# Half of x turned ahead of the last products at three borders, and two orders changed in the first mixer

## The reference

```python
# first block, layers l = 0, 1
mod = silu(c) @ w_ada[l] + b_ada[l]                    # six vectors of 1024: shift, scale, gate, twice
h = rms_norm(x, norm_mix[l]) * (1 + scale_m) + shift_m
x = x + gate_m * hybrid_mixer(h, w_in[l], ..., w_out[l])   # stick-breaking attention and gated linear attention
h = rms_norm(x, norm_ffn[l]) * (1 + scale_f) + shift_f
x = x + gate_f * hierarchical_moe(h, ...)              # 32 experts, top 2 of the best group
# second block, layers l = 0, 1
h = rms_norm(x, norm1_g[l])
x = x + concat(mla, diff, window, neighborhood attention of h @ w_in[l]) @ w_out[l]
h = rms_norm(x, norm2_g[l])
x = x + square(relu(h @ w_up[l])) @ w_down[l]
# at the end
return rms_norm(x, final_norm_g)
```

## Time and profile before

| | us |
|---|---|
| median of 3 runs | 1474.45 |
| lowest, highest | 1472.7, 1476.99 |
| profiled execution | 1473.16 |
| its span, first to last instruction | 1471.0 |
| PE busy in it | 1314.5 (89%) |
| DVE busy | 729.7 (50%) |
| ACT busy | 526.3 (36%) |
| moved by DMA | 392.08 MB |

### The profile page before, as it was taken

One profiled execution on the slowest core, in us unless ns is written; L12 is line 12 of the kernel. 1 busy time (PEld: TensorE's weight loads), 2 busy tenths in 40 slices (PEclk: granted clock), 3 DMA queues, 4 the chain that ended last, 5 costly groups with the idle time before them and its releaser, 6 DMA issues. The chain is left out here.

```text
span 1471.0 us, 21544 instructions
## 1 busy us (share of the span) xinstructions
PE 1314.5 (89%) x9066; PEld 978.5 (67%) x9066; DVE 729.7 (50%) x1126; ACT 526.3 (36%) x894; POOL 49.7 (3%) x46
## 2 busy tenths in 40 slices
PE   5999997866689999976776999999999999999997
PEld 2766774433347667642432878789998978799986
DVE  1744652211157367421111777765545777765554
ACT  3535331000045344200001546553443546644343
POOL 0200000000002000000000110000000110000000
PEclk9999999898799999998878999999999999999999
DMA  9798899999977958999999705455655405455551
GB/s 353 289 334 306 313 422 419 421 421 421 384 286 286 336 206 322 415 420 422 421 378 413 193 10 175 144 173 188 201 191 159 107 14 188 144 172 193 183 199 42
DMA packets 135976, 392.08 MB, mean 267 GB/s; under 512 B 26817, under 2 KB 40129, under 8 KB 111297
## 3 DMA queue, kind: packets, MB, share of 16 engines
q1 hardware_dynamic: 132128, 389.48, 71.1%
q10 hardware_dynamic: 3744, 1.15, 0.4%
HBM read 389.45 MB, written 1.05 MB: 265 GB/s over the span
## 5 line engine op out<-in xcount | busy, mean ns | idle before, releaser
L419 DVE TENSOR_TENSOR spl<-ring,spl 128x2048 fp32r<-128x2048 f32 x65 | 149.0, 2292 | 135.7 <-ACT spl L410 135.7
L543 PEld LDWEIGHTS ps<-hh,spl 128*128 128x128 f32 x1728 | 204.1, 189 | 6.9 <-issue 5.8
L543 PE MATMUL ps<-hh,spl 128*128 128x256 f32 x1728 | 206.2, 280 | 2.8 <-DVE hh L505 2.8
L410 ACT ACTIVATE spl<-ring 128x2048 fp32r<-128x2048 f32 x66 | 126.6, 1919 | 148.4 <-PE ps L543 107.8
L2343 PE MATMUL ps<-spl,ur 128*128 128x512 f32 x768 | 176.7, 389 | 0.0
L2343 PEld LDWEIGHTS ps<-spl,ur 128*128 128x128 f32 x768 | 143.2, 188 | 29.2
L1344 PE MATMUL ps<-ring,ar 128*32 128x256 f32 x928 | 99.4, 444 | 57.1 <-issue 24.2
L932 DVE TENSOR_TENSOR spl<-ring,spl 128x1024 fp32r<-128x1024 f32 (+2 forms) x120 | 138.2, 1175 | 23.3 <-ACT spl L923 22.9
L1344 PE MATMUL ps<-spl_as_slots,ar 128*32 128x256 f32 x864 | 106.8, 497 | 42.1 <-DMA spl_as_slots<-in_w_up 27.1
L923 ACT ACTIVATE spl<-ring 128x1024 fp32r<-128x1024 f32 (+2 forms) x120 | 116.7, 1010 | 44.3 <-PE ps L523 10.7
L523 PE MATMUL ps<-spl,hh 128*128 128x512 f32 x480 | 117.7, 398 | 4.5 <-DVE spl L932 2.1
(11 more groups left out here) (370 smaller groups left out, 1753.8 us busy)
## 6 DMA issues: line engine op xcount, KB each, us to landing
ring<-in_w_up SPq DMA_DIRECT2D x52, 1024.0 KB, 5.3
spl_as_slots<-in_w_down SPq DMA_DIRECT2D x50, 1024.0 KB, 15.2
ring<-in_w_ada SPq DMA_DIRECT2D x48, 1024.0 KB, 7.5
spl_as_slots<-in_w_up SPq DMA_DIRECT2D x40, 1024.0 KB, 16.6
ring<-in_w_gate SPq DMA_DIRECT2D x38, 1024.0 KB, 17.2
ring<-in_w_down SPq DMA_DIRECT2D x38, 1024.0 KB, 4.9
ring<-in_w_in SPq DMA_DIRECT2D x34, 1024.0 KB, 7.3
ring<-in_w_out SPq DMA_DIRECT2D x16, 1024.0 KB, 8.4
```

The source lines that it names most:

```text
L410: sc.activation(t.hi, t.raw, ACT.Copy).then_inc(s_hi, 2)
L419: v.tensor_tensor(t.lo, t.raw, t.hi, ALU.subtract).then_inc(s_lo, 1)
L543: ins = pe.matmul(ps[:, banks[m // 2], (m % 2) * 256:(m % 2) * 256 + 256], le, ri, start=(kk == 0 and q == 0 and m % 2 == 0), stop=(kk == ...
```

## The change

The order strings: in the first mixer, PE's `5155345053` becomes `5134055553` and ACT's `6350054` becomes `0063554` (DVE's is unchanged). In mixer 2 of layer 1, PE's begins with `0040004` in place of `0400040`. The first moves the first half of the ninth tile ahead of the two steps of modulation block 9 on PE, the second its split ahead of three other ACT steps. In `tiles_mix1`, `tiles_cols` is written out, and block 9's tiles come between the two tiles of block 4.

The diff without these strings and without the removed `tiles_cols`:

```diff
@@ -274,13 +270,17 @@
...
             for n, c in enumerate(IN1):
-                tiles_cols(("in", l, c), win, 512 * c, 512)
+                for half in range(2):
+                    tile(("in", l, c, half), [rows(win, 512 * c, 512, 4 * half, 4)], 4, 512)
+                    if l == 0 and n == 4 and half == 0:
+                        tiles_ada(0, [9])
...
                         out_tile(b - 10)
-                    tiles_ada(al, [b])
+                    if (al, b) != (0, 9):
+                        tiles_ada(al, [b])
@@ -480,8 +480,10 @@
...
 
-        def pe_x_T(pe, event):
-            for k2 in range(4):
+        FIRST, LAST = (0, 1), (2, 3)
+        def pe_x_T(pe, event, part=FIRST + LAST):
+            for k2 in part:
@@ -490,28 +492,42 @@
...
 
-        def act_hT(sc, g, gain, last, n):
-            for k2 in range(4):
+        def act_hT(sc, g, gain, part=FIRST + LAST, shift=0):
+            for k2 in part:
...
                 for k in (2 * k2, 2 * k2 + 1):
-                    ins = sc.activation(hT[0][:, k, :], ps[:, k2, k % 2 * 256:k % 2 * 256 + 256], ACT.Identity, scale=gain[:, k:k + 1])
+                    ins = sc.activation(hT[0][:, (k + shift) % 8, :], ps[:, k2, k % 2 * 256:k % 2 * 256 + 256], ACT.Identity, scale=gain[:, k:k + 1])
                 ins.then_inc(s_st, 1)
-            act_hi(sc, last, n)
-        def dve_hT(v, g, gain, last, n):
-            for k2 in range(4):
+        def dve_hT(v, g, gain, part=FIRST + LAST, shift=0):
+            for k2 in part:
...
                 for k in (2 * k2, 2 * k2 + 1):
-                    ins = v.scalar_tensor_tensor(hT[1][:, k, :], ps[:, k2, k % 2 * 256:k % 2 * 256 + 256], gain[:, k:k + 1], hT[0][:, k, :],
+                    h = (k + shift) % 8
+                    ins = v.scalar_tensor_tensor(hT[1][:, h, :], ps[:, k2, k % 2 * 256:k % 2 * 256 + 256], gain[:, k:k + 1], hT[0][:, h, :],
...
                 ins.then_inc(s_hT, 1)
-            if n:
-                dve_lo(v, last, n)
-        def pe_cols(pe, g, key, cn, banks, fresh=False):
+        def pe_cols(pe, g, key, cn, banks, fresh=False, early=False):
...
                 t = T[(*key, half)]
+                if fresh and early and half == 0:
+                    for k, i in ((0, 0), (1, 0), (0, 1), (1, 1), (2, 0), (3, 0), (2, 1), (3, 1)):
+                        if i == 0 and k % 2 == 0:
+                            pe.wait_ge(*g(s_hT))
+                        if (k, i) == (0, 1):
+                            pe.wait_ge(s_staged, 2)
+                        if i == 0 and k == 2:
+                            pe.wait_ge(s_lo, t.m + 1)
+                        pr = parts3([u[:, k, i * 128:(i + 1) * 128] for u in hT], [u[:, k, :] for u in t.parts])
+                        for q, (le, ri) in enumerate(pr):
+                            ins = pe.matmul(ps[:, banks[i], 0:cn], le, ri, start=(k == 0 and q == 0), stop=False, skip_group_check=True)
+                        if (k, i) == (3, 0):
+                            yield
+                    ins.then_inc(s_used, 1)
+                    yield
+                    continue
@@ -529,16 +545,18 @@
...
 
-        def pe_colsT(pe, g, key, banks, fresh=False):
+        def pe_colsT(pe, g, key, banks, fresh=False, shift=0, event=None):
...
                 for m in range(4):
+                    if event and half == 0 and m == 2:
+                        pe_x_T(pe, event, LAST)
...
                             pe.wait_ge(*g(s_hT))
-                        pr = parts3([u[:, k, m * 128:(m + 1) * 128] for u in t.parts], [u[:, kk, :] for u in hT])
+                        pr = parts3([u[:, k, m * 128:(m + 1) * 128] for u in t.parts], [u[:, (kk + shift) % 8, :] for u in hT])
@@ -722,7 +740,7 @@
...
                 lane = pe_colsT(pe, g, ("in", l, 3), [sink_bank(n, 0), sink_bank(n, 1)], fresh=(n == 0)) if c == 3 else pe_cols(
-                    pe, g, ("in", l, c), 512, [sink_bank(n, 0), sink_bank(n, 1)], fresh=(n == 0))
+                    pe, g, ("in", l, c), 512, [sink_bank(n, 0), sink_bank(n, 1)], fresh=(n == 0), early=(l == 0))
@@ -1800,6 +1818,8 @@
...
                 for m, (cols, o) in enumerate(chunks):
+                    if l and n == 0 and half == 0 and m == 2:
+                        pe_x_T(pe, 6, LAST)
@@ -1828,6 +1848,8 @@
...
                     for i in range(2):
+                        if t == 3 and c and i:
+                            pe_x_T(pe, 5 + 2 * l, FIRST)
@@ -1955,8 +1977,8 @@
...
         def pe_mix2(pe, g, l):
-            pe_x_T(pe, 4 + 2 * l)
             if l == 0:
+                pe_x_T(pe, 4)
@@ -2083,9 +2105,12 @@
...
             last = T["up2", l, 0, 1]
-            act_hT(sc, g, PR(f"n1{l}"), last, 1)
+            act_hT(sc, g, PR(f"n1{l}"), LAST if l else FIRST + LAST)
+            act_hi(sc, last, 1)
...
             for c in range(2):
+                if c:
+                    act_hT(sc, g, PR(f"n2{l}"), FIRST, 4)
@@ -2270,7 +2295,8 @@
...
             dve_ms(v, g, (3, 1))
-            dve_hT(v, g, PR(f"n1{l}"), last, 0)
+            if l == 0:
+                dve_hT(v, g, PR("n10"))
@@ -2279,6 +2305,8 @@
...
             v.tensor_reduce(m2.lam[:, 0:2], m2.tl.rearrange("p (a b) -> p a b", b=32), AX.X, ALU.add).then_inc(s_dl, 1)
+            if l:
+                dve_hT(v, g, PR("n11"), LAST)
@@ -2293,6 +2321,7 @@
...
                     else:
+                        dve_hT(v, g, PR(f"n2{l}"), FIRST, 4)
@@ -2322,12 +2351,12 @@
...
         def pe_mlp(pe, g, l):
-            pe_x_T(pe, 5 + 2 * l)
...
                         pe.wait_ge(s_up2, 8 * l + c - 1)
-                    run(pe_colsT(pe, g, ("up2", l, c), [4 + 2 * (c % 2), 5 + 2 * (c % 2)], fresh=(c == 0)))
+                    run(pe_colsT(pe, g, ("up2", l, c), [4 + 2 * (c % 2), 5 + 2 * (c % 2)], fresh=(c == 0), shift=4,
+                                 event=0 if c else 5 + 2 * l))
@@ -2337,6 +2366,8 @@
...
                             for i in range(2):
+                                if l == 0 and d == 7 and f2 and cc and i:
+                                    pe_x_T(pe, 6, FIRST)
@@ -2348,7 +2379,8 @@
...
             last = T["down2", l, 7, 1]
-            act_hT(sc, g, PR(f"n2{l}"), last, 1)
+            act_hT(sc, g, PR(f"n2{l}"), LAST, 4)
+            act_hi(sc, last, 1)
@@ -2371,12 +2403,15 @@
...
                 for i, c in scatter_order:
+                    if (i, c) == (0, 1):
+                        act_hT(sc, g, PR("n11"), FIRST)
...
             last = T["down2", l, 7, 1]
-            dve_hT(v, g, PR(f"n2{l}"), last, 1)
+            dve_hT(v, g, PR(f"n2{l}"), LAST, 4)
+            dve_lo(v, last, 1)
@@ -2400,6 +2435,8 @@
...
                     else:
+                        if l == 0:
+                            dve_hT(v, g, PR("n11"), FIRST)
...
                     v.scalar_tensor_tensor(xs, ps[:, 2 * c + i, :], st[:, 8 + i:9 + i], xs, ALU.mult, ALU.add).then_inc(s_x, 1)
```

More of the change, by code:

```diff
@@ L25 @@
 IN1 = (0, 1, 3, 2, 4, 5)
-ORDER = {("mix1", 0, "PE"): "00400400066550500556650155301535005500515534505314540151315050543510455510404545050055044500000", ("mix1", 0, "ACT"): "0000040660004056645103500061563500543100153113156000135051005640040504400", ("mix1", 0, "DVE"): "00006006040606664065666510630004650031040513141600450044004653415400440044500",
+ORDER = {("mix1", 0, "PE"): "00400400066550500556650155301535005500513405555314540151315050543510455510404545050055044500000", ("mix1", 0, "ACT"): "0000040660004056645103500061500635543100153113156000135051005640040504400", ("mix1", 0, "DVE"): "00006006040606664065666510630004650031040513141600450044004653415400440044500",
          ("mix1", 1, "PE"): "04040000055665000506650215055035053014552531205520045103451415623241005342140255410125000445300020040", ("mix1", 1, "ACT"): "000400040660054066005006153005600315453113601000131530100105640400044", ("mix1", 1, "DVE"): "000400604600606660656660060051304000651431645034104001450403604104404004405",
          ("mix2", 0, "PE"): "0400040040001230010210310243101241234023120413242132401423421031203101213230131420023130132124030023240034201", ("mix2", 0, "ACT"): "00405005000500120031032414102413521523424142031200300101230230141504233201014153402300200344024", ("mix2", 0, "DVE"): "050044000050540123012310550121034024121313242253142414235401400341202312153021153300542132014503102332424311000032220144003",
[1 row of a table removed]
[1 row of a table added]
 def layout(parts):
@@ L255, in tile @@
             T[key] = t
-        def tiles_cols(key, wap, c0, cn):
-            for half in range(2):
-                tile((*key, half), [rows(wap, c0, cn, 4 * half, 4)], 4, cn)
         def tiles_ada(l, blocks):
```

## The result

The changed kernel takes 1481.09 us (median of 14 runs, 1476.1 to 1485.51), the kernel before beside it 1473.35 (14 runs). The ratio is 1.0036, with a 95% interval of 1.0020 to 1.0051: slower by about 5.3 us (the two medians themselves lie 7.7 apart). I had forecast no measurable difference, at 1473.9, with a range up to 1477.4. The profiled execution took 1479.77 us with a span of 1477.6, which is 6.6 more than before. So each trace stands near its kernel's median. Single executions of one kernel lie up to some 8 us apart, so the traces are read stage by stage.

A forecast was written before the change was run, and what follows sets the result against it. It took PE to bound the mixers and MLPs, and DMA bytes the expert blocks. Terms -1.08 + 1.41 - 0.60 + 1.05 - 1.30 = -0.5 us gave a median of 1473.9, range 1470.4 to 1477.4.

The forecast's parts named there:

- part 2: First mixer, ninth projection tile ahead of modulation block 9: 2.12 us wait removed, some 2.7 us added ahead of L867; +1.41 us.
- my condition: First mixer, sign of being right: a gap of 2.5 to 3.5 us ahead of L867 (now L885).
- harmless: First mixer, SP's queue: one modulation load now waits for the ninth tile's subtraction, 104.5 instead of 105.6, without cost.
- just covered: First mixer: next modulation load waits for a step ending at 110.0, not 105.5; needed at 118.0, median transfer 7.5.
- Rival A: First mixer: DMA issues from ACT are cheap and don't delay L985 and L1020; 2.7 us less, 1471.2; chance 0.13.
- Part 1: First tile of the first mixer: PE starts on half a tile and the first staged pair; -1.08 us.
- rival C: First mixer: the first tile's gain is swallowed by loads running back to back; +0.6, 1475.0; chance 0.10.
- Border one: Mixer 2 to MLP, layer 0: PE waits 0.65 us for the second add, 0.25 more later; -0.60 us.
- Border three: Into the MLP of layer 1: no wait for the second add; -1.30 us.
- Border two: MLP to mixer 2, layer 1: -1.30 us, then PE waits 2.35 for the late split (L419); +1.05 us.
- Rival D: ACT's queue passes its whole delay on, first mixer and border two; gap over 3.5 us decides; +1.6, 1476.1; chance 0.20.

The follow-up runs named there:

- e6: Changed kernel with ScalarE's two head copies and low-rank copy ahead of the modulation copy and its four DMA issues; median 1475.29, ratio 1.0008 against before.
- e4: Kernel before with only the first tile of the first mixer taken half by half; median 1472.48, ratio 0.9993 against before.
- e1: Changed kernel with the ninth tile's move taken back (load order and both order strings); median 1475.90, ratio 1.0010 against before.
- e3: Kernel before with the changes at the three borders alone; median 1475.28, ratio 1.0012 against before.
- e5: Changed kernel with TensorE products that nothing reads filling both new waits of the ninth tile; median 1477.96, ratio 1.0025 against before.
- e14: The kernel of e5 run again; no median given, clock at 1.00 from 105 to 130 us.
- e7: Kernel of e1 with the split of layer 1's second in2 tile earlier at border two; median 1473.89, ratio 0.9996 against before.
- e11: Kernel before with eight extra transposes in the midst of each MLP's first up2 block; border one 1.63 us longer, border three 0.94.
- e8: Kernel before with TensorE stopped for its own last product ahead of each up2 block but the first two; median 1479.19, ratio 1.0035.

## Why the prediction was wrong

**Failed: part 2, "What follows on PE is the same work", and with it the price of +1.41 us.** The work is the same, but it ran at 1.2 GHz. I priced a wait by its length. In the first trace the waits cost 0.78 us (from -0.97 to -0.19) and the products behind them 4.13 (from -0.19 to +3.94), with PE busy all the time: 4.9 in all, for a forecast of 1.41. In the two later traces the sum of both was 2.7 and 3.5 us with one and two steps, of which 1.6 and 2.7 were the lower clock. The clock had been at full speed everywhere in the first mixer of before. It was at 0.66 in the earlier trace rows, a stretch with long idle times, and at 0.50 behind the wait of 2.01 us at 875.65. From that I could have asked what a new wait of 2.7 us does to it; I named no such rival. The Trainium skill describes it in "TensorE: Matmul & The Clock Gate", section "HAM oscillation — how this bites in real kernels": groups of products with a wait for DMA between them each start at the lower clock. The trace agrees in kind, with 1.55 us for the four products behind the wait against 0.71; the waits in the page's example are longer than the 1.21 and 2.31 us here.

**Right in part 2:** the cause and place of the wait. The tile started without one, ScalarE's copy and four issues held L1038 up, and PE waited ahead of L885 for L1216 (2.31 us, forecast 2.7, my condition 2.5 to 3.5). Everything there came 1.6 us earlier than I had it, because the tile's products began at 104.36 and not at 105.92. The wait of 1.21 us, for a modulation tile, lay in what I had called "harmless": its load was issued at 103.05 and landed at 110.29, and PE was there at 109.21, earlier than in my sum. The load that I had called "just covered" was covered: issued at 108.41, landed at 113.70, used at 118.65. Rival A was not at work: L1038 stood behind the four issues, and e6, with the issues behind the head copies, takes the wait away. For it I had said that the trace disagrees with the Trainium skill, "DMA: Bandwidth & Descriptors", section "Issuing engines are not separate DMA queues". The page only calls the start of a DMA usually small relative to the DMA itself, and with that the trace agrees. An issue takes 0.62 us here, and its DMA a median of 5.8 us from issue to landing; what delayed L1038 was four issues in a row on ScalarE's queue.

**Part 1, right:** -0.97 for a forecast of -1.08, and e4 keeps it (-0.94 in its trace; ratio 0.9993, -1.0 us). Nothing speaks for rival C, but e4's interval (0.9983 to 1.0003) doesn't exclude it.

**Border one, mis-sized:** forecast -0.60, measured +0.12 (e1 +0.08, e3 +0.06). The wait for the second add came, 0.51 for 0.65. The term that I left out is the pace, 0.84 us. The kernel of e5 shows the border without it: in both its traces (e5 and e14) the 168 products ran at 113.3 ns (19.30 us), and the border gave -0.67 and -0.60. **Border three:** forecast -1.30, measured -0.64, with the same term; no wait, as forecast. **Border two, right:** forecast +1.05, measured +1.22 (+1.02 and +1.03 in e1 and e3), with a wait of 2.08 for 2.35; e7 removes exactly that. Its wait has the clock's price too in 5 of 8 traces, some 1.6 us each; the changed kernel's first trace is one of the three without.

**The sum** of the measured places without the products at 1.2 GHz is -0.97 + 0.78 + 0.12 + 1.22 - 0.64 = +0.5 us, inside the range; with their 4.13 it is +4.6, beside the 5.3 of the medians' ratio. So the term that put the result outside the range is the clock, which had none in the sum. In the trace 1.9 us more come from the places that the change doesn't touch. Rival D's side was right and its mechanism wrong: the gap ahead of L885 stayed under its 3.5 us. The range was too narrow, since each of its ends was a queueing delay.

## What to carry to other kernels

Price a new idle stretch of TensorE in a busy part twice: its length, and the products behind it at 1.2 GHz until the clock is granted again, here 1.6 us for each step. When a step is moved, look at every queue for what its copies and DMA issues now stand ahead of: one changed place in ScalarE's order (e6) gave back 4.1 us, where the whole change had been meant to win 0.5. Where single executions differ by several microseconds, read the stages against each other and profile the kernel again before a step is put down to the change.

## What was not expected of the hardware

- The granted clock fell in steps of 3 to 3.5 us also where TensorE was 100% busy (e3: 196 to 199, 581.5 to 585, 1199.5 to 1202.5 us), in some executions and not in others. The one near 1200 us cost about 1.6 us (e3: +1.63 between 1158 and 1211 us); for the other two no cost shows (+0.28 from 124 to 453 us in e3).
- Products of 128 x 256 at a clock of 1.00 run 113.3 or 117.7 ns apart and keep the pace for whole blocks. Eight transposes in the midst brought the slower one in 10 of 12 traces at border one and in 11 of 12 at border three (e11 shows both cases in the kernel before). Neither a stop of PE (e8) nor the wait of 2.08 us at border two decides it: behind that wait the products ran at 117.7 ns in the changed kernel and at 113.3 in e1. What does is open.
